# Attention and matrix-memory value projections through other PSUM banks, with the first attention step placed between the two halves of the values

## The reference

```
proj = xn @ w_in                       # 512 x 1024 @ 1024 x 3072
qa, ka, va, qd, kd, vd = split(proj)   # va, vd: the values, 512 x 512 each
out_sb  = stick_breaking(qa, ka, va)   # exp(log_sigmoid(z) + sums of log_sigmoid(-z) over later keys) @ va
out_dil = dilated(qd, kd, vd)          # softmax over three dilated windows @ vd
```

## Time and profile before

| | us |
|---|---|
| median of 3 runs | 2630.55 (2625.78 to 2641.48) |
| the profiled execution's own time | 2630.42 |
| span of its profile | 2628.6 |
| mean granted TensorE clock | 0.969 |
| PE busy | 2527.5 (96%) |
| POOL, DVE, ACT busy | 1293.3, 1049.9, 983.6 |

### The profile page before, as it was taken

How to read it: one execution, slowest core, us unless ns; L and a number is a source line. 1 busy time by engine, 2 the same in 40 slices (tenths; PEclk the granted TensorE clock), 3 DMA queues, 4 the chain that set the end, 5 groups by cost and what they waited for, 6 DMA issues and landing times.

```text
span 2628.6 us, 31222 instructions
## 1 busy us (share of the span) xinstructions
PE 2527.5 (96%) x11446; PEld 2045.9 (78%) x11446; DVE 1049.9 (40%) x1590; ACT 983.6 (37%) x1325; POOL 1293.3 (49%) x681
## 2 busy tenths in 40 slices
PE   8999999999999999999999899999999998988997
PEld 6888887755888888888888777678888887867676
DVE  3222323055522211422231650545222693724875
ACT  5333332277533333433333333434333433233543
POOL 5555545400455554555554543225555545256873
PEclk9999999989999999999999899989999998999998
DMA  3333432300233333233333222012333455332741
GB/s 136 96 96 97 146 122 91 90 15 1 64 104 96 97 102 104 80 96 96 96 104 110 67 88 82 23 32 89 96 96 97 143 157 163 108 91 80 187 127 64
DMA packets 79993, 251.64 MB, mean 96 GB/s; under 512 B 9731, under 2 KB 14211, under 8 KB 79788
## 3 DMA queue, kind: packets, MB, share of 16 engines
q1 hardware_dynamic: 72384, 235.55, 28.9%
q10 hardware_dynamic: 6684, 11.90, 1.4%
q0 software_dynamic: 848, 3.15, 0.4%
HBM read 237.54 MB, written 15.25 MB: 96 GB/s over the span
## 4 chain that ended last, share of the span: by engine, by line
PE 76%; issue 9%; POOL 7%; DVE 4%; ACT 2%; DMA 2%; SPq 0%; POOLq 0%; DVEq 0%; ACTq 0%
PE banks L1824 21%; PE banks L1825 21%; PE banks L1826 21%; POOL wl_sb L387 5%; DMA raw_sb<-weights 2%; PE banks L1897 1%; PE banks L1902 1%; PE banks L1898 1%; POOL xl_sb L418 1%; PE banks L1770 1%; DVE x_sb L2173 1%; PE banks L883 1%; PE banks L649 1%; PE banks L874 1%; PE banks L606 1%
## 5 line engine op out<-in xcount | busy, mean ns | idle before, releaser
L387 POOL TENSOR_TENSOR wl_sb<-raw_sb,wh_sb 128x1024 fp32r<-128x1024 f32 x401 | 973.2, 2429 | 1025.8 <-ACT wh_sb L379 1023.4
L1824 PE MATMUL banks<-xh_sb,wh_sb 128*128 128x512 f32 x2064 | 810.9, 393 | 21.1 <-POOL wl_sb L387 13.8
L1825 PE MATMUL banks<-xh_sb,wl_sb 128*128 128x512 f32 x2064 | 806.2, 391 | 0.0
L1826 PE MATMUL banks<-xl_sb,wh_sb 128*128 128x512 f32 x2064 | 805.9, 390 | 0.0
L379 ACT ACTIVATE wh_sb<-raw_sb 128x1024 fp32r<-128x1024 f32 x401 | 424.7, 1059 | 809.8 <-DMA raw_sb<-weights 796.0
L1824 PEld LDWEIGHTS banks<-xh_sb,wh_sb 128*128 128x128 f32 x2064 | 389.4, 189 | 114.1 <-issue 17.7
L1826 PEld LDWEIGHTS banks<-xl_sb,wh_sb 128*128 128x128 f32 x2064 | 389.2, 189 | 81.9
L1825 PEld LDWEIGHTS banks<-xh_sb,wl_sb 128*128 128x128 f32 x2064 | 389.8, 189 | 80.1 <-issue 0.2
L1824 PE MATMUL banks<-hh_sb,wh_sb 128*128 128x512 f32 x704 | 273.9, 389 | 0.0
L1825 PE MATMUL banks<-hh_sb,wl_sb 128*128 128x512 f32 x704 | 273.9, 389 | 0.0
L1826 PE MATMUL banks<-hl_sb,wh_sb 128*128 128x512 f32 x704 | 273.9, 389 | 0.0
(11 more groups left out here) (374 smaller groups left out, 2710.1 us busy)
## 6 DMA issues: line engine op xcount, KB each, us to landing
raw_sb<-weights SPq DMA_DIRECT2D x404, 512.0 KB, 3.5
park<-xs_sb ACTq DMA_DIRECT2D x12, 512.0 KB, 3.5
mix_sb<-scratch SPq DMA_DIRECT2D x16, 258.0 KB, 5.4
hf_sb<-scratch SPq DMA_DIRECT2D x16, 258.0 KB, 5.4
mix_sb<-park SPq DMA_DIRECT2D x4, 1024.0 KB, 6.5
scratch<-scratch ACTq DMA_DIRECT2D x1, 2560.0 KB, 11.8
scratch<-mix_sb SPq DMA_DIRECT2D x8, 259.5 KB, 2.8
x_sb<-x_in SPq DMA_DIRECT2D x8, 256.0 KB, 8.7
```

Source lines behind the costliest of these rows:

```text
L387: pool.tensor_tensor(wl[:, slot, :], raw[:, slot, :], wh_f[:, slot, :], ALU.subtract).then_inc(w_split, 1)
L1824: pe.matmul(dst, wh[:, q, cols], in_hi, start=first, stop=False)
L1825: pe.matmul(dst, wl[:, q, cols], in_hi, start=False, stop=False)
L1826: return pe.matmul(dst, wh[:, q, cols], in_lo, start=False, stop=last)
```

## The change

Attention: both halves of the values go to banks 4 to 7 (`high_banks`). The first half no longer waits for the q and k tiles in banks 0 to 3 (its wait is for a count 12 below the section's base). Then PE issues the logits and scores of unit 0 except score 3, then the second half of the values, whose four tiles wait one by one for the first half's tiles, then waits for all eight tiles, issues score 3 (bank 4), and goes on with unit 0's suffix sums. On ACT the two mask copies move into the q and k section, the first half's copies stay where they were, and the second half's four `high_part` calls and its copies stand within unit 0, after `exps(0, 2)` and ahead of `weights_of(0, 1)`.

Matrix memory: the second half of the values goes to banks 5, 6, 7 and 3. ACT takes out the tile of bank 3 first in each half, and the second half starts when one tile of the first is out. The output gate's eight blocks are written out one by one; the first three use banks 0 to 2 and wait for nothing of the second half; the gate columns (bank 6) come after the first block instead of before it.

```diff
+        V_BANKS = (5, 6, 7, 3)
+        def values_out(act, half):
+            act.wait_ge(blocks_done, BLK["attn.v"] + 4 * half + 4)
+            act.wait_ge(tiles_freed, FREE0 + TILE["attn.v"] + 4 * half)
+            for t in range(4):
+                act.activation((va, vd)[half][:, t, :], banks[:, 4 + t, :], ACT.Copy,
+                               scale=rate_pre[:, t:t + 1]).then_inc(tiles_freed, 1)
         def attention_in_scalar(act):
             for c in range(16):
                 if c:
                     high_part(act, "attn.qk", c % 4, c - c % 4)
-            for half, dst in enumerate((va, vd)):
-                ...
+                if c == 4:
+                    act.wait_ge(mask_loaded, 16)
+                    act.wait_ge(xn_ready, SPLIT["attn"] + 8)
+                    act.activation(ident_r, ident, ACT.Copy).then_inc(mask_turned, 1)
+                    act.activation(later_r, later_mask, ACT.Copy).then_inc(mask_turned, 1)
+            for s in range(4):
+                high_part(act, "attn.v", s, 0)
+            values_out(act, 0)
             def logits_and_scores(u):
                 if u == 0:
-                    pe.wait_ge(tiles_freed, FREE0 + TILE["attn.v"] + 8)
+                    pe.wait_ge(tiles_freed, FREE0 + TILE["attn.v"])
...
-                score(u, 3)
+                if u:
+                    score(u, 3)
...
+            value_tiles(0)
             for u in range(UNITS + 1):
                 if u < UNITS:
                     logits_and_scores(u)
+                if u == 0:
+                    value_tiles(1)
+                    pe.wait_ge(tiles_freed, FREE0 + TILE["attn.v"] + 8)
+                    score(0, 3)
                 if u:
                     both_values(u - 1)
...
                     exps(u, 2)
+                    if u == 0:
+                        for s in range(4):
+                            high_part(act, "attn.v", s, 4)
+                        values_out(act, 1)
                     weights_of(u, 1)
...
-                for t in range(4):
-                    act.activation(mv[:, t, T * half:T * (half + 1)], lin[t], ACT.Copy).then_inc(tiles_freed, 1)
+                for t in (3, 0, 1, 2):
+                    act.activation(mv[:, t, T * half:T * (half + 1)], banks[:, V_BANKS[t] if half else t, :],
+                                   ACT.Copy).then_inc(tiles_freed, 1)
...
+            def token_major(name, half, dst, freed):
+                for b in range(4):
+                    pe.wait_ge(w_split, BLK[name] + 4 * half + b + 1)
+                    for kk in range(2):
+                        k = 2 * b + kk
+                        for t in range(4):
+                            if k == 0:
+                                pe.wait_ge(tiles_freed, FREE0 + TILE[name] + freed[t])
...
+            def attention_values(half):
+                token_major("attn.v", half, high_banks, [-12] * 4 if half == 0 else [1, 2, 3, 4])
...
-            token_major("attn.v")
-            attention_tensor(pe)
+            attention_tensor(pe, attention_values)
...
-            token_major("mlstm.v")
-            gate_columns_tensor(pe)
-            pe.wait_ge(tiles_freed, FREE0 + TILE["mlstm.o"])
-            linear("mlstm.o")
+            token_major("mlstm.v", 0, lin, [0] * 4)
+            token_major("mlstm.v", 1, [banks[:, b, :] for b in V_BANKS], [1] * 4)
+            for b in range(8):
+                pe.wait_ge(w_split, BLK["mlstm.o"] + b + 1)
+                pe.wait_ge(tiles_freed, FREE0 + TILE["mlstm.o"] + (b - 3 if b > 2 else -4))
+                block_mm(pe, lin[b % 4], b % 4, xh, xl)
+                if b == 0:
+                    pe.wait_ge(tiles_freed, FREE0 + TILE["mlstm.o"])
+                    gate_columns_tensor(pe)
```

More of the change, by code:

```diff
@@ L568, in attention_in_scalar @@
                     high_part(act, "attn.qk", c % 4, c - c % 4)
-            for half, dst in enumerate((va, vd)):
[L570 to L573, removed]
-                for t in range(4):
-                    act.activation(dst[:, t, :], lin[t], ACT.Copy, scale=rate_pre[:, t:t + 1]).then_inc(tiles_freed, 1)
+                if c == 4:
[6 more added lines that the diff above has]
+            values_out(act, 0)
         def attention_in_vector(dve):
@@ L599, in score_place, with attention_tensor @@
             return banks[:, SCORE_BANK[j], P:P + n] if j == 1 else banks[:, SCORE_BANK[j], 0:n]
-        def attention_tensor(pe):
+        def attention_tensor(pe, value_tiles):
             q_of, k_of = (lambda u, o=o: qkT[head(u), o + u // 2, :] for o in (0, 4))
@@ L737, in high_of @@
                 act.activation(xh[:, pair + 4 * (bank - 6), :], banks[:, bank, :], ACT.Copy).then_inc(a_oh, 1)
[L739 to L742, removed]
             for u in range(UNITS + 1):
@@ L1918, in linear @@
                         block_mm(pe, lin[s], s, xh, xl)
[L1920 to L1935, removed]
+            def token_major(name, half, dst, freed):
[3 more added lines that the diff above has]
+                        k = 2 * b + kk
+                        cols = slice(kk * T, (kk + 1) * T)
+                        for t in range(4):
+                            if k == 0:
+                                pe.wait_ge(tiles_freed, FREE0 + TILE[name] + freed[t])
+                            tok = slice(t * P, (t + 1) * P)
+                            pe.matmul(dst[t], xh[:, k, tok], wh[:, b, cols], start=(k == 0), stop=False)
+                            pe.matmul(dst[t], xh[:, k, tok], wl[:, b, cols], start=False, stop=False)
+                            last = pe.matmul(dst[t], xl[:, k, tok], wh[:, b, cols], start=False,
+                                             stop=(k == 7))
+                    last.then_inc(blocks_done, 1)
+            high_banks = [banks[:, 4 + t, :] for t in range(4)]
+            def attention_values(half):
+                token_major("attn.v", half, high_banks, [-12] * 4 if half == 0 else [1, 2, 3, 4])
             def ffn(name, idx):
```

## The result

The changed kernel took 2617.09 us (median of 6 runs, 2610.94 to 2621.32) beside 2632.43 for the kernel before: a ratio of 0.9933, interval [0.9914, 0.9951]. Its profiled execution took 2612.31 us (before: 2630.42). Two later sessions timed it again, unaltered: 0.9971 [0.9955, 0.9986] and 0.9962 [0.9945, 0.9978]. So the first was its best session; the three medians lie 15.3, 8.7 and 7.6 us under before's of the same session, 10.5 us on average.

What follows compares the result with a forecast made beforehand. PE was taken to bound the kernel, so only its waits and low-clock time counted. Gains of 9.5 (attention), 1.5, 1.84 and 3.2 us (matrix memory) summed to 16.1: 2630.4 - 16.1 = 2614.3 us, range 2607 to 2623.

Steps and rivals of the forecast that it cites:

- unit 0's 5.1: Attention: unit 0's chain hidden beside the second value half, its work costing 4.99 us instead of 10.08, gain 5.1 us.
- Attention, start and hole: Attention: values start without waiting, gain 0.95 us; the 2.67 us hole between the halves moves to before score 3.
- Attention, the slow stretch behind the hole: Attention, behind the hole before score 3: one half-clock stretch costing 1.6 us, so unit 1 starts at 540.8.
- the second rival: Attention: the hole before score 3 leaves the clock up, 1.6 us more gain, 2612.7 us; chance 0.10.
- The spare on ACT's list: Attention, second value half: block 8 ready at 519.5, wanted by PE at 524.1, spare 4.6 us.
- Memory, locally: Matrix memory's values and output gate: shorter hole 1.5 us, no wait at the gate 1.84, regained clock 3.2.
- Matrix memory, clock: Matrix memory: the half-clock stretches behind the two holes should go, gain 3.2 us, between 0 and 3.4.
- the first rival: Clock not given back, other stretches perhaps low too: memory's 3.2 us lost, attention gives 8.5, 2618.6 us; chance 0.25.

Runs made afterwards that it cites:

- e5_again: The changed kernel run again without a further edit: 2622.44 us beside 2631.1 for the kernel before, ratio 0.9971.
- e12_change_again: The changed kernel timed a third time, without a further edit: 2624.4 us, ratio 0.9962 to the kernel before.
- e9_before: The kernel before, unaltered, profiled a second time: 2628.72 us.
- e7_late_act: The changed kernel with six idle copies (11.6 us) added on ACT before value block 8 of attention is split: 2627.99 us in one execution.
- e8_selector_early: The changed kernel with its two remaining holes filled and POOL's selector copy moved ahead of the output gate's low parts: 2611.93 us, ratio 0.9934 to the kernel before.
- e10_before: The kernel before, unaltered, profiled a third time: 2627.07 us.
- e11_attention_again: The changed kernel without its matrix memory part, timed again: 2622.83 us, ratio 0.9970 to the kernel before.

## Why the prediction was right, and where it was not

**Right in the first session, high by half over all.** 2617.09 lies 2.8 us above the forecast of 2614.3 and in the range; a gain of 16.1 us was forecast, 15.3 came. The medians of the other two sessions, 2622.44 and 2624.4, lie at and just above the range's end of 2623, and both ratios are under 0.5%. The range was made for the mean of the forecast and not for how far sessions differ. That the first session came within 1 us of the forecast gain is partly luck. About half of the 16.1 us was to be regained clock (3.2 in memory, and most of unit 0's 5.1, whose 10.08 us had been at 0.52), and over the whole span clock was regained in the first of three profiles only; there the gains at the places edited, 12.6 and 6.5 us, were larger than forecast, and losses elsewhere made up for it.

**Attention, start and hole: right.** Predicted 0.95 us at the start; the values follow the last q and k matmul in 0.22 us, where it was 1.18. The logits and scores 0 to 2 took 503.32 to 507.66 = 4.34 us (predicted 4.26), the second half began at 507.66 (507.7) without a wait and ended at 529.5 (529.6), and score 3 came at 532.21 (532.3).

**Attention, the slow stretch behind the hole: absent in the first profile, there in the other two.** I took one, for 1.6 us, because three of four such holes had one (one of the three, at 1606.43, was only 1.84 us long and not over 2). In the first profile it didn't come: from 532.21 to 539.26 are 7.05 us at a granted clock of 1.00, so unit 1 started at 539.26 and not 540.8, the second rival's case. In `e5_again` and `e12_change_again`, the same program, it did: behind the same hole of 2.51 us unit 1 came after 8.72 and 8.73 us at 0.80, 1.7 us more. So the forecast's term holds in two of three executions. The kernel before varies as well: `e9_before` has 0.57 from 507 to 511 us, behind the hole at which the first profile had full clock. Which outcome a hole is followed by was not something that one profile could say.

**The spare on ACT's list: right, 6.6 us for 4.6.** The chain on ACT ended at 514.05 and not 515.9: from the exp of the logits to the end of score 2's exponential it took 6.9 us, where 8.6 were taken from a stretch at half clock. The table loads cost what the earlier trace rows show: 505.87 to 507.17 is 1.30 us to the next instruction. The Trainium skill (ScalarE: Activation LUTs, "What ACT_TABLE_LOAD costs") gives 2.66 us for a switch; three such switches would have left almost nothing of the forecast spare, and the trace and the 6.6 us spare in `e7_late_act` decide against that on this path.

**Memory, locally: right.** From the last matmul of the first value half to the last gate matmul it was 73.68 us before and is 67.20 now: 6.48 us, where 1.5 + 1.84 + 3.2 = 6.54 were predicted. The hole is 0.94 us long and the clock behind it 1.00.

**Memory, in the total: wrong.** The step that failed is "Matrix memory, clock. [...] Gain 3.2", together with "What is late next there is only the sigmoid and POOL's copy before the units, untouched." The clock was given back where I looked and taken away one stretch further. Half-clock time in the units, worked out from the granted clock, was 30.7, 23.9 and 23.9 us in three profiles of before; with the memory part, the attention part or both it was 34.1 to 58.0 in all ten used profiles. The shortest of these, `e8_selector_early` with 103.95 us and 34.1 at half clock, is close to the first profile of before. That is what the first rival names ("the shift of everything behind 481 may also put other stretches low"), whether or not the shift is its cause; for it I had worked out too small a price and only from the places edited. What the runs showed in place of the 3.2 is in the sums above: no clock regained over the span. Moreover the first profile had half clock behind both memory holes, and `e9_before` and `e10_before` spend 1.6 us less in that stretch (142.9 and not 144.55), so part of the 3.2 was not there to be won in most executions.

**What stays open.** Why the kernel before has less half clock in the units of memory than every edited version is not settled: attention alone, memory alone and both shift the units by different amounts, and none had the 100 us of `e9_before` and `e10_before`. The instructions right ahead of the units can't be the whole reason, since attention alone has before's there. That the moment at which the stretch comes matters is a guess; no run shifted the units without changing anything else, and what PE did long before them, or the chip, is as open. Nor is it known why blocks 344 to 352 take 64.5 to 64.9 us in the four used profiles without the memory part and 66.4 to 68.2 in the nine with it. PE is busy there 0.9 us more in the first profile of the change and up to 3.3 us more in the others, at a lower clock (0.82 to 0.85 for 0.87); in the first pair it also waits longer for POOL's low parts, 5.3 us for 3.9, but in some of the others it does not.

## What to carry to other kernels

A step whose parts depend on each other through three engines belongs between two long pieces of independent work, not behind them: with its own banks and its inputs already there it costs only its matmuls, here 4.3 us and a score of 0.8 where it was 10.1 us. A clock stretch regained where the profile shows it lost is not a gain until the rest of the span has been measured as well, in several profiles; here the waits that went were kept in full, and regained clock was worth nothing on average. Splitting a profile into PE's idle time and its half-clock time tells the two apart. What paid in the end was to fill more holes: `e8_selector_early`, which filled three more, gained 10.5 us over the change in the same session. Its profile has 5.4 us less idle time than the change's of that session, and 15 us less at half clock; whether the second follows from the first, one profile each can't say.

## What the runs showed of the hardware

- Identical instructions in the units of memory took between 104.75 and 113.00 us in three executions of one program, by granted clock alone (0.84, 0.81 and 0.77 over the stretch): PE's idle time in it was 9.1, 9.2 and 8.8 us.
- A hole of 2.5 us before score 3 was followed by full clock in one execution of the change and by a granted clock of 0.80 in two others of the same program.
- The low clock at 700 to 705 us in the earlier trace rows, with PE busy all the time, moved with its work and did not go: the change has it at 690 to 695, 0.50, and 1.00 at 700 to 705. In both kernels the low clock sets in among the same matmuls of 128 and 1 columns, which count as busy time of PE like any others.

```profile
690.00:695.00 5.00, 5.00 (x22) 0.50 0.00 0
```

```profile
688.85 5.12 PE L1786 MATMUL banks<-inv_d_sb,mix_sb 128*128 128x1 f32 x24
```

- The profiled execution of `e11_attention_again` took 5092.28 us, nearly twice the kernel's time, with PE busy 99% and a granted clock recorded as 1.00 throughout. In 50 us it did 109 matmuls, 0.46 us each, about the length of one at half clock (0.44 in the prediction). ACT was busy 989.8 us, as in the other executions (983.6 before), so only PE was slowed, and the granted clock in the records did not show it. With this execution left out, the median of `e11_attention_again` is 2622.27 us.

```profile
700.00:750.00 50.00, 50.00 (x109) 1.00 0.15 45
```
